# Hybrid diffusion and mixture-of-experts step: the order of turn, down product, scatter and gather in the overflow half-blocks

## What is computed

```python
def _moe(h, router_w, router_bias, w_gate, w_up, w_down):
    x = h.reshape(b * n, d)
    scores = jax.nn.sigmoid(jnp.dot(x.astype(jnp.float32), router_w.astype(jnp.float32)))
    ...
    gates = jnp.sum(jax.nn.one_hot(idx, N_EXPERTS, dtype=jnp.float32) * wsel[..., None], axis=1)
    a = jnp.einsum('td,edf->tef', x, w_gate)
    up = jnp.einsum('td,edf->tef', x, w_up)
    mid = jax.nn.silu(a) * up * gates[:, :, None].astype(x.dtype)
    y = jnp.einsum('tef,efd->td', mid, w_down)
    return y.reshape(b, n, d)
```

## Time and profile before

| | us |
|---|---|
| median of 3 runs | 923.03 |
| the three runs | 923.03, 928.08, 914.71 |
| the profiled execution | 929.42 |
| its span | 927.6 |

### The profile page before, as it was taken

The page is one execution under the profiler, slowest core; times in us unless marked ns, Lnnn a source line. Parts: engine busy times, 40 slices in busy tenths (PEclk is TensorE's granted clock), DMA queues, the critical chain, the costliest instruction groups (busy, mean ns, idle before and its releaser), DMA issues.

```text
span 927.6 us, 11800 instructions
## 1 busy us (share of the span) xinstructions
PE 815.1 (88%) x4207; PEld 464.2 (50%) x4207; DVE 354.3 (38%) x822; ACT 278.6 (30%) x648; POOL 111.1 (12%) x155
## 2 busy tenths in 40 slices
PE   4999999998888995999977799888889998999860
PEld 3456855534443454555535446555554565555430
DVE  3542172454164242422212444664651432322114
ACT  1462122210541152222212436555540332222111
POOL 3400000000000013001023002201200022010120
PEclk8889999999888997999999799989899979999995
DMA  8990233288962266899996956202109379999965
GB/s 276 362 342 11 91 128 105 90 274 279 283 264 92 91 215 233 335 413 410 412 380 215 368 203 228 93 1 93 47 1 346 136 274 320 413 410 411 373 245 207
DMA packets 84182, 219.56 MB, mean 237 GB/s; under 512 B 9526, under 2 KB 19391, under 8 KB 83805
## 3 DMA queue, kind: packets, MB, share of 16 engines
q1 hardware_dynamic: 73822, 197.89, 58.6%
q0 software_dynamic: 8800, 17.38, 5.5%
q10 hardware_dynamic: 1504, 3.56, 1.0%
HBM read 214.18 MB, written 14.83 MB: 247 GB/s over the span
## 4 chain that ended last, share of the span: by engine, by line
PE 69%; DMA 10%; DVE 7%; ACT 4%; issue 4%; DVEq 1%; SPq 1%; POOLq 1%; ACTq 0%; POOL 0%
PE ps L949 61%; DMA arena<-in_moe_w_up_dram 5%; PE ps L956 5%; PE ps L1186 2%; DVEq L1983 1%; DMA h_rows<-xn 1%; DMA xn<-y_rows 1%; DMA hT<-h_rows,rows_in 1%; SPq L703 1%; DMA hT<-h_rows,row_now 1%; DVE xn L2445 1%; DVE negmax L2047 1%; DMA mod_rows<-modrow 1%; PE ps L1200 1%; ACT arena L1634 1%
## 5 line engine op out<-in xcount | busy, mean ns | idle before, releaser
L949 PE MATMUL ps<-arena 128*64 128x256 f32 (+11 forms) x1164 | 236.6, 448 | 23.6 <-POOLq L796 6.8
L949 PEld LDWEIGHTS ps<-arena 128*64 128x64 f32 (+3 forms) x1164 | 128.5, 168 | 112.8 <-issue 65.2
L949 PE MATMUL ps<-ring,hT 128*128 128x512 f32 (+2 forms) x384 | 134.3, 510 | 4.5 <-issue 3.9
L949 PE MATMUL ps<-ring,arena 128*64 128x256 f32 (+1 forms) x784 | 111.3, 431 | 5.3 <-DMA ring<-in_moe_w_down_dram 3.8
L949 PEld LDWEIGHTS ps<-ring,hT 128*128 128x128 f32 x384 | 73.6, 193 | 63.2 <-issue 58.7
L949 PEld LDWEIGHTS ps<-ring,arena 128*64 128x64 f32 x784 | 53.9, 137 | 51.1 <-issue 28.1
L1634 ACT ACTIVATE arena<-ps 128x256 f32<-128x256 f32 (+4 forms) x94 | 42.2, 463 | 89.2 <-PE ps L949 85.6
L956 PE MATMUL ps<-ident,arena 128*128 128x128 f32 (+2 forms) x332 | 51.8, 297 | 16.6 <-DVE hT L2053 4.7
L949 PE MATMUL ps<-hT,ring 128*128 128x384 f32 x192 | 62.1, 486 | 0.0
L956 PEld LDWEIGHTS ps<-ident,arena 128*128 128x128 f32 (+2 forms) x332 | 40.1, 145 | 37.4 <-issue 16.2
L2379 DVE TENSOR_TENSOR arena<-arena,ps 128x128 f32<-128x128 f32 x37 | 10.7, 288 | 124.8 <-ACT arena L1742 124.8
(11 more groups left out here) (312 smaller groups left out, 870.2 us busy)
## 6 DMA issues: line engine op xcount, KB each, us to landing
ring<-in_w_mod_dram SPq DMA_DIRECT2D x48, 1024.0 KB, 8.7
ring<-in_moe_w_down_dram SPq DMA_DIRECT2D x22, 1024.0 KB, 17.0
ring<-in_moe_w_gate_dram SPq DMA_DIRECT2D x38, 512.0 KB, 12.9
ring<-in_moe_w_up_dram SPq DMA_DIRECT2D x38, 512.0 KB, 15.6
arena<-in_moe_w_gate_dram SPq DMA_DIRECT2D x36, 512.0 KB, 9.7
arena<-in_moe_w_up_dram SPq DMA_DIRECT2D x36, 512.0 KB, 11.3
arena<-in_moe_w_down_dram SPq DMA_DIRECT2D x15, 1024.0 KB, 13.9
ring<-in_ev_w_in_dram SPq DMA_DIRECT2D x9, 1024.0 KB, 11.9
```

Of the source, the lines that this page charges most:

```text
L949: mm = pe.matmul(out, lhsT, rhs, **kw)
```

## The change

Four programs are reordered, with the same instructions in each. On TensorE the next block's rows are turned behind the down product, not between the gate and up product and the transpose of mid. On ScalarE and VectorE the row copies (and `row_now`) move behind the result copies. On GpSimd each scatter of an overflow block goes ahead of the gather that stood in front of it; both keep their waits.

```diff
@@ gpsimd, before the loop @@
                 scatter(NPAIR - 1)
+                for half in range(2):
+                    pool.wait_ge(y_read[half][l], NE + 1)
+                pool.indirect_dma_start(y_rows, bass.IndirectOffsetOnAxis(ap=to_now[0:HALF, :], axis=0), ysb[0:HALF, 0, :], None,
+                                        bounds_check=2 * T - 1, oob_is_err=False).then_inc(over_stored[l], 16)
                 pool.wait_ge(row_ready[l], 2)
                 pool.wait_ge(xt_full[1][l], NPAIR + 2)
                 pool.indirect_dma_start(xg_over, None, h_rows[l], ...
...
@@ gpsimd, in the loop @@
                     pool.drain()
+                    pool.wait_ge(over_done[l], b + 1)
+                    pool.wait_ge(y_read[1][l], b + (NE + 1))
+                    pool.tensor_tensor(pool_mark[:, 0:1], ...
+                    pool.indirect_dma_start(y_rows, ...
                     pool.wait_ge(row_ready[l], b + 2)
                     pool.wait_ge(xt_full[1][l], b + (NPAIR + 2))
...
@@ tensor, over_block @@
-                    pe.wait_ge(over_gathered[l], b * 16 + 32)
-                    turn_in(xg_over, None)
                     pe.wait_ge(mt_read[l], b + NE)
                     turn_mid(0, b + (NE + 1))
...
                     mm = down(0, early_w[:, slots[2], :].rearrange("p (j n) -> p j n", n=D))
                     mm.then_inc(y_full[l], 1)
+                    pe.wait_ge(over_gathered[l], b * 16 + 32)
+                    turn_in(xg_over, None)
@@ scalar, over_block @@
                     silu(0)
-                    act.wait_ge(xt_full[0][l], b + (NPAIR + 2))
-                    rows_copy(xgT[:, 0, 0:4, 0:HALF], HALF)
...
                     result(ysb[0:HALF, 0, 0:512], 0, done)
+                    act.wait_ge(xt_full[0][l], b + (NPAIR + 2))
+                    rows_copy(xgT[:, 0, 0:4, 0:HALF], HALF)
@@ vector, over_block @@
                     middle(0)
-                    dve.wait_ge(xt_full[1][l], b + (NPAIR + 2))
-                    rows_copy(xgT[:, 0, 4:8, 0:HALF], HALF)
-                    dve.tensor_copy(row_now[:, :], rows_over[:, bass.ds(b + 2, 1)]).then_inc(row_ready[l], 1)
...
                     result(ysb[0:HALF, 0, 512:], 0)
+                    dve.wait_ge(xt_full[1][l], b + (NPAIR + 2))
+                    rows_copy(xgT[:, 0, 4:8, 0:HALF], HALF)
+                    dve.tensor_copy(row_now[:, :], rows_over[:, bass.ds(b + 2, 1)]).then_inc(row_ready[l], 1)
```

More of the change, by code:

```diff
@@ L876, in _ @@
                     over_gathered[l], 16)
[L877 to L880, removed]
                 nb = blocks_of(pool, l)
@@ L883, in _ @@
                     pool.drain()
+                    pool.wait_ge(over_done[l], b + 1)
+                    pool.wait_ge(y_read[1][l], b + (NE + 1))
+                    pool.tensor_tensor(pool_mark[:, 0:1], pool_mark[:, 0:1], pool_mark[:, 0:1], ALU.mult)
+                    pool.indirect_dma_start(y_rows, bass.IndirectOffsetOnAxis(ap=to_now[0:HALF, :], axis=0), ysb[0:HALF, 0, :], None,
+                                            bounds_check=2 * T - 1, oob_is_err=False).then_inc(over_stored[l], 16)
                     pool.wait_ge(row_ready[l], b + 2)
                     pool.wait_ge(xt_full[1][l], b + (NPAIR + 2))
-                    pool.tensor_tensor(pool_mark[:, 0:1], pool_mark[:, 0:1], pool_mark[:, 0:1], ALU.mult)
+                    pool.tensor_tensor(pool_mark[:, 1:2], pool_mark[:, 1:2], pool_mark[:, 1:2], ALU.mult)
                     pool.indirect_dma_start(xg_over, None, h_rows[l], bass.IndirectOffsetOnAxis(ap=row_now[:, :], axis=0), bounds_check=T - 1, oob_is_err=False).then_inc(
                         over_gathered[l], 16)
[L889 to L893, removed]
                 pool.wait_ge(over_stored[l], nb * 16 + 16)
```

## The result

| | before | after |
|---|---|---|
| median, 20 runs each (us) | 924.75 | 929.62 |
| lowest to highest | 914.71 to 930.58 | 921.94 to 939.65 |
| ratio, with 95% interval | | 1.0066 (1.0038 to 1.0094) |
| the profiled execution's span | 927.6 | 924.3 |

The change costs 0.66% of the time, 6.1 us (3.5 to 8.7). One slow run of the changed kernel (939.65 us) is in its median and not in the ratio; the medians as they stand lie 4.9 us apart, inside that interval. The prediction was 922.3 us, 0.7 us under the 923.03 of the three runs it had; the median of 929.62 lies outside its range of 915 to 929. The two profiled executions stand the other way round, 924.3 against 927.6, and that is a warning: a span of one execution is no measure of 6 us here (more on it at the end).

What follows compares the result with a forecast made beforehand. TensorE was taken to carry the program (69% of the chain). Layer 0's -1.7 us and layer 1's +1.0 gave -0.7: 928.7 us on the profiled execution, 922.3 on the median of 923.03; range 915 to 929.

Steps and rivals of the forecast that it cites:

- (a): All five overflow blocks: gate and up product to down product takes 1.37 us instead of 1.50, 0.13 us saved each.
- (b): Layer 0, row copies behind result copies: block 1's gate and up product starts at 483.35 and ends 1.09 us later.
- (c): Layer 0, block 1: the stall for the gather goes, and the down product ends 3.17 us earlier, at 490.56.
- (d): End of layer 0: the last gather, now behind the scatter, holds ScalarE's y_rows reads until 496.5; layer 0 gains 1.7 us.
- late gather: Rival, chance 0.2: gathers take 8.4 and 7.7 us; layer 0 gains 0.2, layer 1 loses 1.9; 924.7 us.
- (e): Layer 1: last down product gains 0.27 us, the last gather behind the scatter costs 1.3; layer 1 loses 1.0 us.
- Late scatter: Rival, chance 0.15: block 0's scatter in layer 0 takes 8.4 us, not 6.8; layer 0 gains 0.1; 923.9 us.
- Full gain: Rival, chance 0.15: the last gather doesn't hold the y_rows reads; -3.5 us in all, 919.5 us.

Runs made afterwards that it cites:

- second and third profile: The kernel before, unchanged, profiled twice more to see whether layer 0's stall recurs; the two executions took 921.85 and 918.74 us.

## Why the prediction was wrong, step by step

The stretch from anchor to scale, as the median of three profiles before and the mean of two after: 25.61 and 33.87 before, 28.56 and 36.71 after, together 5.8 us longer. The time rose by 6.1 (3.5 to 8.7). Nothing outside the stretch is needed.

(a) Sized 1.37 us from product to down product, measured 477.75 - 476.29 = 1.46, against 1.50 before. Right in kind for a block 0, and next to nothing. In the loop there is no gain at all: from product to down product 1.67 us in block 1 of layer 0 and 1.64 in the last block of layer 1, against 1.64 there before (899.98 - 898.34). I had carried 0.13 us from block 0 to all five blocks.

(b) Right: block 1's product started at 7.40 us behind the anchor, forecast 7.31, and ended 0.95 us later than in the first profile.

(c) The down product came earlier, by 3.0 us of the forecast 3.17, against the first profile. Against the other two it came 1.0 and 1.5 us earlier. They stalled for 1.5 and 1.9 us, not 2.6, and their transposes took 1.09 us. The slow matmuls were a fact of the first execution: behind its stall the granted clock was 0.58 in the transposes (third number from the end) and 0.73 in the down product.

```profile
488.75:490.50 1.75, 1.75 (x9) 1.55 (x9) 0.00 (x0) 0.38 (x1) 0.00 (x0) 0.58 0.81 335
```

I had sized the whole gain on one profile of a transfer under load, and its spread from execution to execution was in none of my cases.

(d) "The last scatter follows down by 1.94 us" failed. It was issued at 18.10 us, where the steps gave 16.5, because the drain holds GpSimd. The page of before had no word of it, but the line's own group in that trace did:

```profile
L883 POOLq DRAIN  x3: 4182/5412/6993, 484.4 to 895.0; - x3
```

The first drain starts at 484.4 and takes 6.99 us, so it ends at 491.4. The scatter before it landed at 483.69 + 6.8 = 490.5. After the change it reads:

```profile
L883 POOLq DRAIN  x3: 3309/4827/8337, 483.1 to 889.4; - x3
```

483.1 + 8.34 = 491.4 again, and the gather ahead of it landed at 490.58. In both kernels it ends some 0.9 us behind the landing. So in layer 0 the last scatter is set by a landing and not by the down product, 17.63 and 18.12 us before (second and third profile), 18.10 and 17.84 after: the whole gain of TensorE's part is lost there. The last gather follows it, and ScalarE's reads start 21.6 and 21.4 us behind the anchor, where the forecast had 20.5 and the late gather 22.0.

(d) and (e) "The first tile needs both, and ScalarE's took 4.96" is the step that made most of the loss. I let the read keep its length while it started 1 us after the other half. It took 7.1 and 6.6 us, 2.1 and 1.6 more, in both layers. Its start came 0.8 us later in layer 0 (21.5, against 20.70) and 1.4 in layer 1 (30.1, against 28.71). 2.1 + 1.6 + 0.8 + 1.4 is 5.9, the 5.8 of above but for medians and rounding. The start in layer 1 was forecast 1.0 later than in the first profile and measured 1.02, but by luck: the down product gained nothing where 0.27 was forecast (the 1.64 of (a)), and from its end to the reads it took 5.5 us and not 5.8.

Gathers behind scatters landed after 7.6 us in layer 0 (I took 6.8) and 3.9 in layer 1 (I took 5.1). The late gather didn't come about in layer 1, whose transposes never waited; in layer 0 its start of the reads was nearer than the forecast's. Late scatter didn't come about. Full gain had its sign wrong: it supposed that a late half has the queues to itself.

The range was built on the spread of runs round a shift of -0.7 us, with cases to +1.7 us. The shift was 6, and no case held it, since no case priced a read that is overtaken.

## What to carry to other kernels

When two transfers that end one step are let go at different times, the later one isn't late by the difference alone: reads 1 us apart cost 2 to 3.5 us in each layer here. Ask of every wait in front of an issue whether that transfer needs it, and move the rest of the wait behind the issue. Before a stall is priced as a gain, ask whether what it waits for is needed at all, look at it in a second execution, and look whether the engine that comes next has a drain or another hold of its own that ends at the same time.

## What the runs showed of the hardware

- Reads that start together share the pace, and reads that start 1 us apart don't. The issues of layer 1, windows 900:902.5 after the change and 906:908 before (KB each, median us to landing):

```profile
arena<-y_rows SPq DMA_DIRECT2D x3, 512.0 KB, 4.6
xn<-y_rows ACTq DMA_DIRECT2D x3, 512.0 KB, 7.5
```

```profile
arena<-y_rows SPq DMA_DIRECT2D x3, 512.0 KB, 6.6
xn<-y_rows ACTq DMA_DIRECT2D x3, 512.0 KB, 7.3
```

SP's three became 2.0 us quicker, about as quick as where ScalarE's start 3.8 us later (4.5 us, layer 0 without the drain), and ScalarE's didn't gain from it. The Trainium skill, page DMA: Bandwidth & Descriptors, section Queues, rings and completion order, has each engine take turns between the queues. By even turns the late half's first tile would still have landed about as long after its own start as before. That is argued and not measured. These runs show the earlier queue favoured; why is open.

- An empty gather lands in 2.1 us with the queues idle, in 8.4 and 7.6 us while weights stream (480.33 before, 483.00 after, layer 0), and in 8.4 us when six reads are issued 0.2 us behind it. It moves nothing. The same section of the Trainium skill says that a completion is written after the earlier writes of its engine in all its queues; the reads here were issued later, so that alone doesn't cover it.

- GpSimd's drain lasts until the indirect DMA ahead of it has landed. In layer 0 it ends 0.9 us behind the landing in the first profiles of before and after, and in the last turn of layer 1 before 0.1 us behind (895.0 + 4.18 = 899.2, against 894.9 + 4.2 = 899.1). Without it the mark came 1.3 us sooner. I had left it out of the sum altogether.

- The granted clock goes with the spread between executions. Over the 20 runs of the changed kernel its correlation with the time is -0.75; 926.13 us goes with 0.941 and 935.77 with 0.927. The stretch from 600 to 700 us, after and then before (the clock is the third number from the end):

```profile
600.00:700.00 100.00, 88.06 (x442) 53.16 (x441) 55.38 (x113) 47.67 (x128) 13.45 (x20) 0.97 0.20 64
```

```profile
600.00:700.00 100.00, 89.42 (x448) 55.64 (x447) 55.47 (x113) 50.15 (x132) 14.18 (x21) 0.91 0.15 48
```

Between the first scale of layer 0 and the anchor of layer 1 the first profile of before took 374.2 us (877.37 - 503.22) and that of after 368.2 (871.24 - 503.08), on the same instructions. These 6.0 us outweigh the change inside the two stretches (4.4 us between these two profiles), and so the slower kernel has the shorter profiled span.
